# One channel tile of a depthwise convolution: computed by GpSimd, with a product and an addition for each tap, in place of TensorE

## The reference

```python
def conformer_conv(h, w_pw1, b_pw1, w_dw, b_dw, ln_g, ln_b, w_pw2, b_pw2):
    u = h @ w_pw1 + b_pw1
    a, gate = jnp.split(u, 2, axis=-1)
    u = a * jax.nn.sigmoid(gate)
    u = lax.conv_general_dilated(          # CONV_WIDTH = 31, causal, one filter to a channel
        u, w_dw[:, None, :].astype(u.dtype), window_strides=(1,),
        padding=((CONV_WIDTH - 1, 0),),
        dimension_numbers=("NWC", "WIO", "NWC"),
        feature_group_count=D_MODEL) + b_dw
    u = jax.nn.silu(layer_norm(u, ln_g, ln_b))
    return u @ w_pw2 + b_pw2
```

## Time and profile before

| | us |
|---|---|
| median of 3 runs | 1249.8 (1246.28 to 1252.29) |
| the profiled execution | 1245.27 |
| its span, first to last instruction | 1243.9 |
| TensorE busy | 1182.7 (95%) |
| VectorE busy | 751.9 (60%) |
| ScalarE busy | 611.5 (49%) |
| GpSimd busy | 58.0 (5%), 85 instructions |

### The profile page before, as it was taken

One profiled execution on the slowest core, in us unless ns is written; L12 is line 12 of the kernel. 1 busy time (PEld: TensorE's weight loads), 2 busy tenths in 40 slices (PEclk: granted clock), 3 DMA queues, 4 the chain that ended last, 5 costly groups with the idle time before them and its releaser, 6 DMA issues.

```text
span 1243.9 us, 17182 instructions
## 1 busy us (share of the span) xinstructions
PE 1182.7 (95%) x7233; PEld 1051.8 (85%) x7233; DVE 751.9 (60%) x929; ACT 611.5 (49%) x833; POOL 58.0 (5%) x85
## 2 busy tenths in 40 slices
PE   6999899998996999999999999999899999999996
PEld 4788889877886998889899998878797888999985
DVE  5843553356666899675465664565667656555542
ACT  5544864454444466455444443455466544434431
POOL 1010000000001000000020000000003001000000
PEclk9999997898997999999999999999999999999999
DMA  9874341323674531354455646555334533564550
GB/s 351 306 234 149 102 154 55 116 85 112 212 236 140 170 136 35 102 169 153 136 161 178 205 162 214 186 185 191 133 98 141 192 130 121 185 204 164 176 186 34
DMA packets 104492, 198.83 MB, mean 160 GB/s; under 512 B 3873, under 2 KB 18305, under 8 KB 104416
## 3 DMA queue, kind: packets, MB, share of 16 engines
q1 hardware_dynamic: 100864, 186.46, 44.7%
q0 software_dynamic: 3552, 11.29, 3.0%
HBM read 196.69 MB, written 1.05 MB: 159 GB/s over the span
## 4 chain that ended last, share of the span: by engine, by line
PE 71%; DVE 13%; ACT 10%; issue 2%; DMA 2%; POOL 1%; SPq 0%; DVEq 0%; ACTq 0%; POOLq 0%
PE product L526 61%; DVE w_low L483 5%; ACT w_high L474 4%; PE small L2069 3%; PE small L557 2%; DMA w_raw<-in_w_ada 1%; PE small L1381 1%; PE small L1702 1%; ACT drows L2576 1%; ACT H_high L570 1%; PE small L1210 1%; DVE drows L2656 1%; DVE stats L2658 1%; PE small L1723 1%; DMA sink_row<-in_sink 1%
## 5 line engine op out<-in xcount | busy, mean ns | idle before, releaser
L483 DVE TENSOR_TENSOR w_low<-w_raw,w_high 128x2048 fp32r<-128x2048 f32 (+3 forms) x184 | 404.2, 2203 | 252.6 <-ACT w_high L474 244.5
L474 ACT ACTIVATE w_high<-w_raw 128x2048 fp32r<-128x2048 f32 (+3 forms) x184 | 338.0, 1841 | 181.2 <-PE product L526 151.2
L526 PE MATMUL product<-H_low,w_high 128*128 128x256 f32 x1088 | 312.7, 287 | 7.8 <-DVE H_low L577 5.9
L526 PE MATMUL product<-H_high,w_high 128*128 128x256 f32 x1088 | 310.7, 286 | 0.0
L526 PE MATMUL product<-H_high,w_low 128*128 128x256 f32 x1088 | 310.2, 285 | 0.0
L526 PEld LDWEIGHTS product<-H_low,w_high 128*128 128x128 f32 x1088 | 211.2, 194 | 11.4 <-issue 7.9
L526 PEld LDWEIGHTS product<-H_high,w_low 128*128 128x128 f32 x1088 | 211.3, 194 | 0.3
L526 PEld LDWEIGHTS product<-H_high,w_high 128*128 128x128 f32 x1088 | 211.1, 194 | 0.0
L526 PE MATMUL product<-w_high,H_low 128*128 128x512 f32 (+4 forms) x416 | 159.7, 384 | 4.0 <-ACT k_b L828 2.3
L526 PE MATMUL product<-w_high,H_high 128*128 128x512 f32 (+4 forms) x416 | 158.1, 380 | 0.0
L526 PE MATMUL product<-w_low,H_high 128*128 128x512 f32 (+4 forms) x416 | 157.5, 379 | 0.0
(11 more groups left out here) (366 smaller groups left out, 1601.6 us busy)
## 6 DMA issues: line engine op xcount, KB each, us to landing
w_raw<-in_ffn_w_gate SPq DMA_DIRECT2D x20, 1024.0 KB, 5.1
w_raw<-in_ffn_w_up SPq DMA_DIRECT2D x20, 1024.0 KB, 5.2
w_raw<-in_ffn_w_down SPq DMA_DIRECT2D x20, 1024.0 KB, 5.1
w_raw<-in_w_merge SPq DMA_DIRECT2D x16, 1024.0 KB, 5.1
w_raw<-in_w_ada SPq DMA_DIRECT2D x12, 1024.0 KB, 6.5
w_raw<-in_w_in SPq DMA_DIRECT2D x12, 1024.0 KB, 5.4
w_raw<-in_mem_w_k SPq DMA_DIRECT2D x8, 1024.0 KB, 5.1
w_raw<-in_conv_w_pw SPq DMA_DIRECT2D x16, 512.0 KB, 5.0
```

Of the source, the lines that this page charges most:

```text
L474: k.act.eng.activation(chunk_view(k, k.w_high[j], i), chunk_view(k, k.w_raw[i % k.N_RAW], i), ACT.Copy).then_inc(*k.act.tells("weights_hig ...
L483: k.vec.eng.tensor_tensor(low, raw, high.bitcast(F32), ALU.subtract).then_inc(*k.vec.tells("weights_low", ("weights low", i)))
L526: mm = pe.eng.matmul(bank[:, off:off + wide], a, r, start=b not in started, stop=True, skip_group_check=True)
```

## The change

Of the three channel tiles of TensorE's way one goes to GpSimd. The tiles are numbered anew: VectorE 0, 1, 3, 4, 5, GpSimd 2, TensorE 6 and 7. VectorE has five tiles as before. On GpSimd each tap is two instructions: a product into one of two new buffers (`tap_product0` and `tap_product1`) and an addition to `conv_out`; the first tap's product carries the bias and goes there directly. The product of the next tap is issued ahead of this tap's addition. With fewer groups of taps on TensorE there are 8 rounds in place of 12, and VectorE takes 13 steps in each in place of 10. The means take TensorE's tiles first, then GpSimd's, then VectorE's.

```diff
@@ -415,6 +415,7 @@
         self.variance = self.sb("ln_variance", [P, S])
+        self.tap_products = [self.sb(f"tap_product{i}", [P, S]) for i in range(2)]
@@ -2023,11 +2024,10 @@
-ON_PE = 3
-VEC_TILES, PE_TILES = list(range(KT - ON_PE)), list(range(KT - ON_PE, KT))
+VEC_TILES, POOL_TILE, PE_TILES = [0, 1, 3, 4, 5], 2, [6, 7]
 TAP_GROUPS = [(f, range(g, min(g + 4, TAPS))) for f in PE_TILES for g in range(0, TAPS, 4)]
-ROUNDS = ON_PE * (1 + TAPS // 8)
+ROUNDS = len(PE_TILES) * (1 + TAPS // 8)
@@ -2041,6 +2041,27 @@
     k.norms["mem", 0].pool_gain()
+    g.wait_ge("taps", ("glu", POOL_TILE))
+    y, made = k.conv_out[:, POOL_TILE, :], {}
+
+    def product(tap):
+        src, wt = k.conv_in[:, POOL_TILE, tap:tap + S], k.taps[:, POOL_TILE, tap:tap + 1]
+        if tap == 0:
+            g.eng.tensor_scalar(y, src, wt, k.vcol["b_dw"][:, POOL_TILE:POOL_TILE + 1], ALU.mult, ALU.add).then_inc(*g.tells("taps_pool"))
+        else:
+            g.wait_ge(added.get(tap - 2))
+            g.eng.tensor_scalar(k.tap_products[tap % 2][:, :], src, wt, 1.0, ALU.mult, ALU.mult).then_inc(*g.tells("taps_pool"))
+        made[tap] = g.last
+
+    added = {}
+    product(0)
+    product(1)
+    for tap in range(1, TAPS):
+        if tap + 1 < TAPS:
+            product(tap + 1)
+        g.wait_ge(made[tap], added.get(tap - 1, made[0]))
+        g.eng.tensor_tensor(y, y, k.tap_products[tap % 2][:, :], ALU.add).then_inc(*g.tells("taps_pool", ("conv out", POOL_TILE)))
+        added[tap] = g.last
     root = k.stat("ln root", NT)
@@ -2088,7 +2109,7 @@
-    order = PE_TILES + VEC_TILES
+    order = PE_TILES + [POOL_TILE] + VEC_TILES
@@ -2256,7 +2277,7 @@
-        steps(vec_taps, 10)
+        steps(vec_taps, 13)
```

## The result

| | before | after |
|---|---|---|
| median | 1250.25 us (1246.28 to 1252.29) | 1264.35 us (1260.73 to 1265.06) |
| ratio | | 1.0111, interval 1.0079 to 1.0142 |
| the profiled execution | 1245.27 us | 1260.73 us |
| its span | 1243.9 us | 1259.3 us |
| TensorE, VectorE, GpSimd busy | 1182.7, 751.9, 58.0 us | 1177.0, 768.7, 110.0 us |

The sign and the mechanism were forecast, and the time lies in the range; the loss of 14.1 us is less than half of the 29 us named.

What follows compares the result with a forecast made beforehand. VectorE was taken as late next once TensorE is relieved: 30.5 us of holds put the means 28.5 us later, and TensorE's clock adds 2.5, together +31.0 on 1245.27 us. Forecast 1279 us, range 1254 to 1304 us.

Steps and rivals of the forecast that it cites:

- What bounds: Convolution before the means: VectorE is late next, so TensorE's 13.4 us give at most 1.2 us plus the bias addition.
- rival C: VectorE's taps after 424.9 us: not held, they keep 0.40 us; +0.6 us, 1250 us by the median; chance 0.15.
- third bias addition: VectorE, for TensorE's removed tile: 0.4 us less, so its tiles alone would end at about 500.7 us.
- GpSimd's own speed: GpSimd's tile: 61 instructions of 0.55 us, 34 us, ending alone at 459 to 475 us.
- The hold: VectorE's taps beside GpSimd: each of 61 instructions holds VectorE some 0.5 us, 30.5 us in all.
- the forecast's case: VectorE and GpSimd each in turn: a delay of 15 to 40 us, 1264 to 1290 us; chance 0.58.
- What comes behind: TensorE after VectorE's last tile: the means begin at 531.2 us and not 502.66, +28.5 us; nothing behind takes it back.
- The clock: TensorE's restart after over 40 us of idleness, at the lower clock level: +2.5 us.
- The signs I named: Trace during GpSimd's tile and before the means: longer VectorE taps, GpSimd waits, one TensorE wait, clock 0.5, 62 ScalarE diagonals.
- GpSimd starving: Port never free between VectorE's taps, GpSimd mostly works after them until 541 us: +38 and 2.5, 1290 us; chance 0.10.
- Dearer turns: GpSimd's turns at 0.70 us plus 0.1 us each: 49 us of VectorE delay, 1299 us by the median; chance 0.17.
- VectorE not held: The same case as rival C: GpSimd streams beside VectorE's next tap; +0.6 us, 1250 us; chance 0.15.

Runs made afterwards that it cites:

- no_pool_taps: The changed kernel with GpSimd doing only the first tap of its tile: 1248.59 us against 1249.38 for the kernel before, ratio 0.9993.
- sums_in_psum: The changed kernel with VectorE's running sums in PSUM, only a tile's last tap writing to SBUF: 1250.38 us against 1248.34 for the kernel before, ratio 1.0008.
- vector_quiet2: The changed kernel without taps 1 to 30 of VectorE's five tiles, their places in the order kept: 1237.64 us, one execution.
- psum_two_pool_tiles: The changed kernel with VectorE's sums in PSUM and tiles split VectorE four, GpSimd two, TensorE two: 1252.49 us, ratio 1.0043 to the kernel before.

## Why the prediction was right in kind and too large

**What bounds.** Right. VectorE was late next, and TensorE's 13.4 us brought nothing (no_pool_taps: 0.9993). The case without a hold (rival C) was priced at +0.6 us. It measured 0.9 us under before with GpSimd idle (no_pool_taps) and 1.0 us over it with GpSimd at work (sums_in_psum), both within the noise. One detail of the sum was wrong: 0.4 us were taken off VectorE's last tap for the third bias addition, but that one stands behind the last tap already.

**GpSimd's own speed.** Right in size: 0.55 us an instruction was taken as a duration, and 0.48 and 0.74 us are the records, 0.64 us on average from start to start. The addition is nearer to the estimate of 0.6 to 0.75 us that the prediction gave beside its sum. GpSimd started at 426.05 us and ended at 481.43 us; forecast for GpSimd on its own were 459 to 475, and with the 48.9 us of vector_quiet2 it would be 475.

**The hold.** This is the step that failed: "each of the 61 instructions holds VectorE for some 0.5 us (the 0.55 less what runs beside the end of a VectorE instruction), 61 x 0.5 = 30.5 us." It was 16.3 us, 0.27 us each: 0.17 for a product, 0.44 for an addition. The turns are there, one for one; but I set the hold nearly equal to the duration. That the time still lies in the range is owed to the wide bounds: 17.1 us of delay stand near the lower edge of the 15 to 40 us of the forecast's case. A GpSimd instruction on 2 columns took 0.19 us; taken as a fixed part that holds nobody, it would have given 61 x 0.19 = 11.6 us less, 19 us in place of 30.5. The runs bear such a part out: of a product's record 0.48 - 0.17 = 0.31 us held nobody, of an addition's 0.74 - 0.44 = 0.30. Why it is 0.3 us and not 0.19 stays open. By the Trainium skill (SBUF — State Buffer, Who interferes with whom) the pair of ports is kept for the whole instruction; the runs show a hold of 38% of a product's and 52% of an addition's time from start to start, so taken at its word the rule overstates the cost. What the same section says besides, that an instruction of VectorE with at most one SBUF input, outside the two-port modes, doesn't contend, is what sums_in_psum shows: 0.44 us a tap with one, 0.74 with two.

**What comes behind.** I let TensorE begin all sixteen records of the means after the last tap. It took the tiles as they came; only the last six records were left (2.93 us at the lower clock), and the end of the means lay 2.2 us after the last tap, 5.0 before. Forecast was a gain of 1.6 us here; it was 2.8, and 4.4 without the clock: at full clock six of these records take 6 x 3.45/16 = 1.3 us, 1.6 less than they took.

**The clock.** Forecast +2.5 us. TensorE did run at the lower level (granted clock 0.69 and 0.82 on average in the two stages above, between levels of 0.50 and 1.00), and it cost nearly as much: those 1.6 us in the means, and 0.4 in the weight piece behind them, which took 5.99 us against 5.58. That is some 2.0 us.

The sum by its own terms: 17.1 (last tap) - 4.4 + 2.0 = 14.7 us, against 30.1 - 1.6 + 2.5 = 31.0. Of the 17.1 us 16.3 are the hold; the other 0.9 are there in no_pool_taps too. The sum was too high by 13.0 us for the last tap, 2.8 for the means and 0.5 for the clock. The spans differ by 15.4 us, of which 1.3 lie before the stage (424.04 against 425.37) and 0.6 are won back behind it; the medians differ by 14.1.

**The signs I named.** Taps from 0.40 towards 0.9 us and back: yes (0.74). GpSimd's 0.55 us "and the wait for VectorE's on top": no, its pair grew only from 1.28 to 1.50 us. One wait of TensorE of 35 to 50 us: no, three of 20.0 us together. ScalarE's diagonals 62: yes. I had written that TensorE's weight products would be ready and it would reach 489.3 us; VectorE was late for the gated product as well, and 11.6 us of the waiting came there.

**The rivals.** GpSimd starving: refuted, it finished at 481. Dearer turns: refuted. VectorE not held: refuted as the cases stand, and true as soon as the sums lie in PSUM.

## What to carry to other kernels

Work put on an idle GpSimd is paid for in part by VectorE where VectorE's instructions read two SBUF tensors: here 0.17 us for each product and 0.44 us for each addition on 256 columns, 16.3 us in all, and the 13.4 us taken from TensorE gave nothing for it. Before such a move see which engine ends next, and whether its operands can lie elsewhere: with VectorE's running sums in PSUM the same tile cost nothing that shows (1.0008, 0.9991 to 1.0026). Then the gain has still to be dealt out, since what one engine saves is worth nothing while the other ends when it did: only with 16 taps handed back to TensorE did the tile on GpSimd bring 0.5%.

## What the runs showed that I had not expected

- VectorE's tap costs no more with its sum in PSUM: 0.44 us in pairs, as in SBUF, and 52 in a row took 20.45 us against 20.68.
- GpSimd's product of 256 columns has a record of 0.48 us and its addition one of 0.74; from 2 columns (0.19 us) that is 1.1 ns a column and 2.2, where the rows of before suggested 2 for both.
- The long holds are GpSimd's: a 2.28 us subtraction of VectorE's holds it for nearly all its length (a product of 2.65 us), while in the other direction the subtraction grew to 2.81 us at most in the changed kernel, and to 3.9 us in psum_two_pool_tiles.
- A product by a scalar on VectorE from SBUF to SBUF is held too, although it reads one tensor: three took 2.11 us beside GpSimd in the changed kernel and 1.05 before. The Trainium skill (SBUF — State Buffer, Who interferes with whom) says that such an instruction can enter a mode that uses the shared pair; no run here takes that mode apart. From SBUF to PSUM, in sums_in_psum, three took 1.43 us beside GpSimd, 0.48 each, and two before GpSimd's start 0.99.
- Two tiles of VectorE's taps in turn run at 0.44 to 0.46 us a tap, three at 0.40.
